# Norm sums with ones as the stationary operand and the squares as the moving one, the per-token sums read from the product's diagonal by VectorE

## The reference, cut to what matters

```
D_MODEL = 1024; SEQ = 256; DEPTH = 2; EPS = 1e-6

def _rms(x):
    xf = x.astype(jnp.float32)
    return xf * lax.rsqrt(jnp.mean(xf * xf, axis=-1, keepdims=True) + EPS)

for layer in range(DEPTH):
    sh1, sc1, g1, sh2, sc2, g2 = jnp.split(mod, 6, axis=-1)
    hmix = rms_norm(x, norm_mix[layer]) * (1.0 + sc1) + sh1
    proj = hmix @ w_in[layer]
    ...  # attention | retention | SSM on slices of proj, merged
    x = x + g1 * (merged @ w_out[layer])
    hffn = rms_norm(x, norm_ffn[layer]) * (1.0 + sc2) + sh2
    x = x + g2 * peer(hffn, peer_w_q[layer], peer_subkeys[layer], peer_u[layer], peer_v[layer])
return rms_norm(x, final_norm)
```

## Time and profile before

| | us |
|---|---|
| median of 3 runs | 2117.64 |
| lowest and highest of them | 2114.34, 2126.79 |
| the profiled execution | 2111.2 |
| its span, first to last instruction | 2109.4 |
| PE busy | 2024.2 (96%) |
| DVE busy | 1572.2 (75%) |
| ACT busy | 1081.3 (51%) |
| POOL busy | 258.5 (12%) |
| mean granted TensorE clock | 0.988 |

### The profile page before, as it was taken

One profiled execution on the slowest core, in us unless ns is written; L12 is line 12 of the kernel. 1 busy time (PEld: TensorE's weight loads), 2 busy tenths in 40 slices (PEclk: granted clock), 3 DMA queues, 4 the chain that ended last, 5 costly groups with the idle time before them and its releaser, 6 DMA issues.

```text
span 2109.4 us, 34074 instructions
## 1 busy us (share of the span) xinstructions
PE 2024.2 (96%) x11188; PEld 1742.2 (83%) x11188; DVE 1572.2 (75%) x3436; ACT 1081.3 (51%) x1703; POOL 258.5 (12%) x309
## 2 busy tenths in 40 slices
PE   4998999999999999999999989999999999999998
PEld 4788989888888888888778989898888888888876
DVE  8883889766788888887656358996676767678854
ACT  3223338654776766666522142585555555554443
POOL 2002439200000000000010043690000000000000
PEclk9999999999999999999999999999999999999998
DMA  9366311355778877555443362114555565555561
GB/s 369 133 261 259 121 54 52 136 180 197 261 290 294 295 280 280 189 180 208 164 168 110 106 244 81 66 64 172 190 188 189 204 214 198 189 188 181 179 233 60
DMA packets 115595, 391.66 MB, mean 186 GB/s; under 512 B 12736, under 2 KB 20800, under 8 KB 115008
## 3 DMA queue, kind: packets, MB, share of 16 engines
q1 hardware_dynamic: 115520, 390.69, 51.9%
HBM read 384.35 MB, written 6.29 MB: 185 GB/s over the span
## 4 chain that ended last, share of the span: by engine, by line
PE 62%; DVE 22%; issue 7%; ACT 3%; DMA 3%; DVEq 1%; SPq 1%; POOL 1%; ACTq 0%
PE ps L868 23%; PE ps L859 12%; PE ps L861 5%; PE ps L613 5%; DVE v_lo L1678 3%; DVE next_w_ada_ring L1723 3%; DVE u_lo L1673 3%; PE ps L626 3%; PE ps L754 2%; DVE onehot_gate L1657 2%; PE ps L830 2%; DMA weight_ring<-in_w_q_dram 2%; DVE gated L1686 2%; ACT gelu L1220 2%; DVE gelu L1682 1%
## 5 line engine op out<-in xcount | busy, mean ns | idle before, releaser
L859 PE MATMUL ps<-h_hi_lo,u_hi 128*128 128x512 f32 x1728 | 629.0, 398 | 8.3 <-DVE u_lo L1673 8.1
L861 PE MATMUL ps<-h_hi_lo,u_lo 128*128 128x256 f32 x1512 | 424.6, 281 | 0.0
L859 PEld LDWEIGHTS ps<-h_hi_lo,u_hi 128*128 128x128 f32 x1728 | 325.2, 188 | 79.0 <-issue 6.5
L861 PEld LDWEIGHTS ps<-h_hi_lo,u_lo 128*128 128x128 f32 x1512 | 286.3, 189 | 8.1
L1673 DVE TENSOR_TENSOR u_lo<-weight_ring,u_hi 128x1024 fp32r<-128x1024 f32 x216 | 263.7, 1222 | 22.0 <-ACT u_hi L1209 18.8
L868 PE MATMUL ps<-v_hi,gated_hi 128*128 128x512 f32 x864 | 272.2, 396 | 5.6 <-DVE gated_lo L1692 4.6
L868 PE MATMUL ps<-v_lo,gated_hi 128*128 128x512 f32 x864 | 268.4, 392 | 0.0
L868 PE MATMUL ps<-v_hi,gated_lo 128*128 128x512 f32 x864 | 266.4, 390 | 0.0
L1678 DVE TENSOR_TENSOR v_lo<-weight_ring,v_hi 128x1024 fp32r<-128x1024 f32 x216 | 263.3, 1219 | 0.5 <-ACT v_hi L1214 0.5
L1214 ACT ACTIVATE v_hi<-weight_ring 128x1024 fp32r<-128x1024 f32 x216 | 227.4, 1053 | 52.8 <-PE ps L868 52.6
L1209 ACT ACTIVATE u_hi<-weight_ring 128x1024 fp32r<-128x1024 f32 x216 | 227.6, 1055 | 4.6 <-DMA weight_ring<-in_u_tab_dram 3.9
(11 more groups left out here) (318 smaller groups left out, 3209.0 us busy)
## 6 DMA issues: line engine op xcount, KB each, us to landing
weight_ring<-in_u_tab_dram SPq DMA_DIRECT2D x224, 512.0 KB, 4.4
weight_ring<-in_v_tab_dram SPq DMA_DIRECT2D x216, 512.0 KB, 3.5
next_w_ada_ring<-in_w_ada_dram SPq DMA_DIRECT2D x56, 512.0 KB, 4.5
weight_ring<-in_w_in_dram SPq DMA_DIRECT2D x46, 512.0 KB, 3.6
w_ada_ring<-in_w_ada_dram SPq DMA_DIRECT2D x40, 512.0 KB, 7.8
v_tail<-in_v_tab_dram SPq DMA_DIRECT2D x40, 512.0 KB, 4.8
weight_ring<-in_w_q_dram SPq DMA_DIRECT2D x32, 512.0 KB, 3.5
u_ahead<-in_u_tab_dram SPq DMA_DIRECT2D x22, 512.0 KB, 8.6
```

What stands on the lines that cost most here:

```text
L859: last = mm(both, UH[:, b, k, :], HB[:, :, k, :], start=(k == 0), stop=(k == KT - 1))
L861: mm(PS[:, 4 + b, 0:T], UL[:, b, k, :], HH[:, k, :], start=False, stop=False)
```

## The change

The sums of squares change their operands. `ONES`, all 128 columns of it, becomes the stationary operand, and a whole tile of squares (256 tokens) the moving one: 8 matmuls per norm instead of 16, each 256 columns wide instead of 1. The product then holds the sum of every token in every partition, 128x256, in one PSUM bank. VectorE takes each token's sum onto its own partition by multiplying each 128x128 half with the identity and adding along the row, with 1/D as scale and EPS as start value; the result goes where the mean + eps went before. The wait for `IDENT` (`in_const`, norm 0 only) moves ahead of it.

Apart from this, semaphores are merged: the two pairs of the mixing stage's roots into one pair that counts twice as far, and the eleven of `u_ahead` into six, one per pair of tiles, so that a tile is waited for together with its neighbour.

```
@@ sum_squares (TensorE) @@
                 for k in ks:
                     pe.wait_ge(squared, n * KT + k + 1)
-                    for t in range(TT):
-                        last = mm(PS[:, bank + t, 0:1], SQ[:, k, t * P:(t + 1) * P], ONES[:, 0:1], start=(k == 0),
-                                  stop=(k == KT - 1))
+                    last = mm(PS[:, bank, 0:T], ONES[:, :], SQ[:, k, :], start=(k == 0), stop=(k == KT - 1))
@@ rms (VectorE) @@
                 bank = 4 * (n % 2)
-                v.tensor_scalar(RS[:, :], PS[:, bank:bank + TT, 0], 1.0 / D, EPS, ALU.mult, ALU.add).then_inc(var_done, 1)
                 if n == 0:
                     dve.wait_ge(in_const, 16)
+                for t in range(TT):
+                    last = v.tensor_tensor_reduce(out=DIAG[:, t, :], in0=PS[:, bank, t * P:(t + 1) * P], in1=IDENT[:, :],
+                                                  scale=1.0 / D, scalar=EPS, op0=ALU.mult, op1=ALU.add,
+                                                  accum_out=RS[:, t:t + 1])
+                last.then_inc(var_done, 1)
                 dve.wait_ge(std_done, n + 1)
@@ semaphores @@
+A_RING = 11
...
-        in_ahead = [sem(f"u_ahead_loaded_{a}") for a in range(A_TOP)]
+        in_ahead = [sem(f"u_ahead_pair_loaded_{a}") for a in range((A_RING + 1) // 2)]
...
+        def ahead_loaded(l, a):
+
+            pair = a % A_RING // 2
+            tiles = [b // A_RING for b in range(A_TOP) if b % A_RING // 2 == pair]
+            return in_ahead[pair], 16 * (l * len(tiles) + sum(b <= a // A_RING for b in tiles))
...
-                            sp.dma_start(RAWU[a][:, :, :], u_tab[l, NM + a].rearrange("p (k n) -> p k n", n=P)).then_inc(in_ahead[a], 16)
+                            sp.dma_start(RAWU[a][:, :, :], u_tab[l, NM + a].rearrange("p (k n) -> p k n", n=P)).then_inc(in_ahead[a // 2], 16)
...
-                    pe.wait_ge(in_ahead[a], 16 * (l + 1))
+                    pe.wait_ge(*ahead_loaded(l, a))
...
-                act.wait_ge(rvar, l + 1)
-                fn(SM[:, 3, :], SM[:, 3, :], ACT.Sqrt).then_inc(rstd_done, 1)
-
-                act.wait_ge(mvar, l + 1)
+                act.wait_ge(mvar, 2 * l + 1)
+                fn(SM[:, 3, :], SM[:, 3, :], ACT.Sqrt).then_inc(mstd, 1)
+
+                act.wait_ge(mvar, 2 * l + 2)
...
-                dve.wait_ge(rstd_done, l + 1)
+                dve.wait_ge(mstd, 2 * l + 1)
                 link(v.reciprocal(SM[:, 3, :], SM[:, 3, :]))
-                dve.wait_ge(mstd, l + 1)
+                dve.wait_ge(mstd, 2 * l + 2)
```

More of the change, by code:

```diff
@@ L262, in trunk @@
         h_hi = sem("h_hi_done")
[L263 to L266, removed]
+        mvar = sem("head_and_merge_var_done")
+        mstd = sem("head_and_merge_std_done")
         h_split = sem("h_split_done")
@@ L1531, in _ @@
                 link(v.reduce_sum(SM[:, 3, :], YSQ, AX.X))
-                v.tensor_scalar(SM[:, 3, :], SM[:, 3, :], 1.0 / HD, EPS, ALU.mult, ALU.add).then_inc(rvar, 1)
+                v.tensor_scalar(SM[:, 3, :], SM[:, 3, :], 1.0 / HD, EPS, ALU.mult, ALU.add).then_inc(mvar, 1)
                 dve.wait_ge(ao_mm, l + 1)
```

## The result

The changed kernel takes 2123.14 us (median of 12 runs, 2118.66 to 2127.26), the kernel before 2113.82 us beside it (12 runs, 2110.46 to 2126.79). The ratio of the two, taken side by side, is 1.0036, with a 95% interval of 1.0025 to 1.0047: slower by 0.4%, some 8 us by the ratio and 9 us by the medians, where 6 us less were forecast. The time is 3 us above the top of the range.

The account below looks back on a forecast made before the run. The chain was taken as 62% TensorE and 22% VectorE. Norm 0 -0.6, norms 1 and 3 +0.1 each, norm 2 -3.4, norm 4 -2.2: about -6.0 us, from median 2117.64 to 2111.6, range 2105 to 2120.

Parts of the forecast that it names:

- the sum's silence on everything outside the norms: The forecast's total counted only the five norms and the semaphores (0): together about -6.0 us.
- VectorE: In the norms, added products with accumulator delay the root: +0.36 us, on the chain in norms 0, 2 and 4.
- Rival (c): The clock falls inside the wide sums; the highest case, 2122.3 us; chance 0.12.
- TensorE at full clock: In the sums, 8 wide matmuls cost 3.5 us, 16 narrow 3.4: no gain; norms 1 and 3 +0.1 us each.
- The clock in norms 2 and 4: Full clock held through the wide sums: 1.6 us gained in norm 2, 2.0 us in norm 4.
- the last 1.6 us: Projection behind norm 2: 16 matmuls take 7.06 us instead of 8.68 if the clock holds over root and spread.
- rival (a): Clock holds through the sums, falls before the projection behind norm 2: -4.4 us, median 2113.2; chance 0.28.
- rival (d): VectorE's products in the norms take 0.58 us instead of 0.36: 0.7 us of gain lost, 2112.3; no separate chance.
- Norm 0: Sums there run at the lower clock; wide ones lift it after 3 to 6 us: net gain 0.6 us.
- Spread: Behind the sums of norms 2 and 4, the spread at full clock takes 0.61 for 1.23 us: 0.6 each.
- Rival (b): Gains in norm 0 and norm 2 hidden by tile transfers, norm 4 alone stays: -2.0 us, median 2115.6; chance 0.13.
- The signs' chances: Whole kernel's time: within 0.5% of no change 0.90, faster by more 0.07, slower by more 0.03.

Follow-up runs that it names:

- the variance in four: Kernel before, with VectorE's variance written as four instructions instead of one, three more per norm: ratio 1.0069, from two executions only.
- TensorE's half: Kernel before with the wide sums in all five norms, VectorE keeping one variance instruction (values not the reference's): ratio 0.9971, 2108.0 us.
- the two of the last experiment: Against the kernel before: wide sums with four VectorE instructions per norm, 0.9979, 2113.7 us; new form in norms 2 to 4 only, repeated, 0.9979, 2111.42 us.
- the late norms the first time: Kernel before with the new form in norms 2, 3 and 4 only, old semaphores, first run: ratio 0.9984, 2110.06 us.

## Why the prediction was wrong

**The step that failed is the sum's silence on everything outside the norms.** Under "VectorE" I priced the added instructions by how long they run (+0.36 us) and on which chain. I gave no price to what they do to the code behind them, and closed the sum with five norms and the semaphores. "A time other than all of the cases, as when the clock's other falls land elsewhere" had 0.05. What the runs showed in its place: six instructions more ahead of the gate loop of layer 0 cost +9.2 us, whatever the instructions are (the changed kernel, the variance in four, six idle memsets), five cost 7.7, and 0, 3, 4 or 12 nothing there. Rival (c), up to 2122.3, comes near the measured 2123.14 only by luck: it counted from a base 3.8 us too high, and what it supposes did not happen: the clock did not fall inside the wide sums of norms 2 and 4 in any of the nine traces that have them. No run shows its 2122.3 us. What the changed kernel shows in its place is the projection behind norm 2, where a wide product, two records, takes 0.85 us from start to start at a clock of 0.50 and 0.43 us at 1.00.

**TensorE at full clock.** Right: 3.69 us for eight wide products, forecast 3.5 to 3.7. In norms 1 and 3 nothing can be told from the spread of that stretch, where the start of the next stage varies by some 3 us between executions.

**The clock in norms 2 and 4.** Right: 1.00 through the sums in both. That wide matmuls hold the clock, on which the 1.6 and 2.0 us of the sums rest, was my assumption, and no run shows why it held; what the runs show is 1.00 through the sums of both norms in all nine traces with the wide form. But the price of the fall was read from one trace, and the other traces of the old form show that it was a dear one. In norm 2 the second trace of the kernel before keeps the full clock through all 32 narrow records, and they take no longer than the wide ones:

```profile
1068.71 3.70 PE L580 MATMUL ps<-ones,squares 128*128 128x1 f32 x32 [0.68 <-ACT squares L1028]
```

Over the seven traces with the old norm 2 its sums take 3.7 to 5.5 us, 4.7 in the mean, against 3.69 in all nine with the new one: about 1.0 us gained there, not 1.6. Over the seven with the old norm 4 they take 3.7 to 5.8, 5.1 in the mean: 1.4 gained, not 2.0. So these two terms are some 1.2 us too large together. Of the last 1.6 us, which divided the forecast from rival (a), the trace after shows the rival: 0.56 at the projection's start. The experiments show that it goes both ways. From the first projection product of layer 1 to its first attention scores, the nine traces with a wide norm 2 have 64.5 to 64.6 us in five (norms 2 to 4 alone, twice; TensorE's half; the changed kernel's second trace; the changed kernel with six memsets) and 66.2 to 67.2 in four; the seven with the narrow one have 66.1 to 67.3 in all. So 0.42 against 0.28 was about fair, and the term's size, 1.6 us, too.

**VectorE.** Right: 0.54 us from the first product to the root, forecast 0.55, so rival (d) is out. The table of the root is loaded in time (1082.24 to 1083.52 us, the root at 1084.01).

**Norm 0.** Right: 0.6 us net, as the forecast's middle, and about where the forecast had the lift: the wide records start 0.43 us apart for the first 3.1 us of the sums and 0.22 behind that (in the second trace of the changed kernel after 3.9), forecast after 3 to 6. That this is the clock is read from the distances alone, as the granted clock stands at 1.00 over all of these sums.

**Spread.** 0.71 us for 1.23, 0.5 gained where 0.6 was forecast, each time.

**Rival (b)**, that the gain is hidden elsewhere: wrong for TensorE's half, which has no VectorE cost and shows about 6 us in the whole time, 0.9971 (0.9959 to 0.9983). For the forms that pay on VectorE it is less clear: 0.9979 for the two of the last experiment, 4.4 us, which is rival (a)'s figure, 0.9984 for the late norms the first time, and 0.9989 (0.9977 to 1.0000), 2.3 us, for the change with one instruction less, whose interval holds rival (b)'s 2.0 us as well.

**The signs' chances.** The interval of the result lies within 0.5%, which had 0.90; it is the range's upper end, 2120, that was too near. It is called rival (c), but lies below that rival's own 2122.3 and the 2126.8 that a run of the kernel before had already shown.

**What stays open.** The gate stage explains 9.2 us. The ratio says +8 against a forecast of -6 (or -4.4), which leaves 3 to 5 us. Some 1.2 us of them are the two terms above that were sized too large. Some 2 us stand in the experts of layer 1: 602.0 to 602.1 us in the two traces of the changed kernel and in that of the norm's edit alone (598.7 in both traces of before, 599.8 to 601.1 in the other kernels). I didn't take that apart. The merged semaphores, priced at 0, may hold some of the rest.

What makes VectorE pause ahead of instruction 650 isn't proved, but the traces say more than that. Around each gate loop, packets of 8 KB run on a queue that the trace calls "instruction" (q14), which by that name would be code that is loaded; the traces do not show what a packet carries. One of them moves with the count of VectorE's instructions ahead of the loop, also in the runs where nothing but VectorE's program differs. In layer 1, where it stands alone near the loop's start, its start behind the loop's first one-hot is:

| instructions more ahead of layer 1's loop | traces | packet starts, us |
|---|---|---|
| 0 | 5 | 4.3 to 4.5 |
| 3 | 1 | 4.0 |
| 5 and 6 | 4 | 3.8 to 3.9 |
| 8 | 1 | 3.7 |
| 12 | 4 | 2.3 to 2.4 |
| 18 | 1 | 1.4 |

In layer 0 it starts at 1.6 to 1.8 us with 0 more, 1.4 with 3 or 4, 1.1 to 1.5 with 5 or 6, and with 12 more 9.5 us ahead of the loop, where the pause is gone from the loop too. So I take it for VectorE's code. The pause ends 0.5 to 0.9 us ahead of the packet's start in each trace that shows one, in layer 1's slow trace as well (0.87 and 1.41 us), so the pause and the packet go together. That the one is the cause of the other is not shown: no run separates it from another cause.

## What to carry to other kernels

Adding or removing instructions on an engine is an edit to all the code behind them: in a loop where VectorE and GpSimd seem to hold each other up, a pause of 0.27 us that came to stand elsewhere was enough here to cost 9.2. So compare the stages that the diff doesn't touch, before and after, first. To test it, put idle instructions where the engine waits anyway, in the old kernel; if that alone brings the loss, the edit is innocent, and a form of it with the old number of instructions keeps the gain. A tuned loop like this one, with 0.01 us between the starts of the two outcomes, can be tipped by a later edit, as here by five or six instructions 300 us ahead of the loop; an explicit wait that fixes the order, or less work of the two engines at one time, might protect it, which no run here tried. And a price for a clock's fall should come from more than one trace: in the kernel before it fell 1.9 us into the sums of norm 2 in one trace and behind their end in the next.

## What the runs showed of the hardware

- VectorE paused at one place of its program, in the first pass of layer 0's gate loop and in no later one, and the place stays with the instruction's number. With 5 or 6 instructions added ahead, the 2nd one-hot started 0.54 us behind the 1st, for 0.26 before (the changed kernel in both its traces, the norm's edit alone, the variance in four, five and six memsets). With 3 or 4 added, the 3rd started 0.45 us behind the 2nd, for 0.26 (norm 1 alone, one instruction less per norm). With 0 or 12 added, the first four started 0.26 us apart.
- A packet on the trace's "instruction" queue (q14) moved with the number of VectorE's instructions: from 4.3 to 4.5 us behind the start of layer 1's loop with 0 added to 1.4 us with 18 added.
- In the first pass of a gate loop, GpSimd's first one-hot of 128 columns beside VectorE's wide ones took 0.59 to 0.65 us where the order held. Where it tipped, this one-hot took 1.89 to 1.90 us in three traces (the changed kernel, the norm's edit alone, six memsets), 1.21 in two (the changed kernel's second trace, the variance in four) and 1.10 in layer 1 of the changed kernel with six memsets; with five memsets the order tipped in the second pass, with 1.13. From there on the loop stayed slow for all the passes left (six or seven), by 1.3 us each.
- With ones as the stationary operand and 256 columns moving, the granted clock stood at 1.00 through the 3.69 us of the sums in norms 2 and 4 of all nine traces (18 of 18). With the one-column form it fell to 0.50 inside the sums, 1.2 to 3.2 us in, in 11 of 14, and behind their end in the other three. Between the sums of norm 2 and the projection, with the spread in the middle, the clock stayed at 1.00 in five of the nine.
- A wide product of the projection took 0.43 us from start to start at a granted clock of 1.00 and 0.85 us at 0.50 (the changed kernel, 1087 to 1096 us).
- In the changed kernel a product with an accumulator over 128 columns took 288 ns in the mean (285 to 293) and its read 82 to 84; two pairs took 0.54 us from their start to the start of the root behind them.
